# A decoder layer on one core: the order of six branch products, two earlier weight slots, one split inside a norm, and the last scatter

## The reference, cut to what matters

```python
h = rms_norm(x, g_mix)
rq, rk, rv, rg, mq, mk, mv, cq, gl = split(h @ w_in)
o_ret  = rms_norm(retention(rq, rk * RET_DK**-0.5, rv), g_ret_out) * silu(rg)
o_moba = moba_attention(rms_norm(mq), rms_norm(mk), mv)         # 256 tokens: one causal block, ALiBi
mk_, mv_ = split(rms_norm(mem, g_mem) @ w_mem_kv)
o_mem  = softmax(rms_norm(cq) @ rms_norm(mk_).T * MEM_HD**-0.5) @ mv_
gates = sigmoid(gl + b_gate)
y = gates[0] * (o_ret @ w_br_ret) + gates[1] * (o_moba @ w_br_moba) + gates[2] * (o_mem @ w_br_mem)
x = x + y @ w_out

xt = rms_norm(x, g_ffn)
top_v, top_e = top_k(xt @ w_router + b_router, 4); wts = softmax(top_v)
# for each expert e, on the tokens that chose it:
hdn = xt @ w_mlp1[e] + b_mlp1[e]
glu, lin = min(hdn[::2], 7), clip(hdn[1::2], -7, 7)
out = x + sum over e of wts * ((glu * sigmoid(1.702 * glu) * (lin + 1)) @ w_mlp2[e] + b_mlp2[e])
```

## Time and profile before

| | |
|---|---|
| time, median of 3 runs | 1188.52 us (1187.39 to 1189.92) |
| time of the profiled execution | 1189.44 us |
| span of the profiled execution | 1187.5 us |
| TensorE busy | 1147.0 us (97%) |
| VectorE busy | 403.0 us (34%) |
| ScalarE busy | 227.3 us (19%) |
| GpSimd busy | 30.3 us (3%) |
| DMA | 454.86 MB, mean 383 GB/s |
| mean granted TensorE clock | 0.991 |

### The profile page before, as it was taken

The page is one execution under the profiler, slowest core; times in us unless marked ns, Lnnn a source line. Parts: engine busy times, 40 slices in busy tenths (PEclk is TensorE's granted clock), DMA queues, the critical chain, the costliest instruction groups (busy, mean ns, idle before and its releaser), DMA issues.

```text
span 1187.5 us, 13156 instructions
## 1 busy us (share of the span) xinstructions
PE 1147.0 (97%) x5377; PEld 540.3 (45%) x5377; DVE 403.0 (34%) x664; ACT 227.3 (19%) x353; POOL 30.3 (3%) x31
## 2 busy tenths in 40 slices
PE   9999999999999999999999999999999999999998
PEld 8788778874333333333333333333333333333332
DVE  4765666854222222223222322222222222222221
ACT  3545556531000000001011000000000000000001
POOL 0000222100000000000000000000000000000000
PEclk9999999999999999999999999999999999999999
DMA  9765444899999999999999999999999999999996
GB/s 350 273 207 187 151 157 153 317 422 403 421 434 429 432 427 432 430 429 432 429 429 429 429 429 430 428 432 430 428 433 427 428 431 430 427 429 426 429 426 258
DMA packets 46050, 454.86 MB, mean 383 GB/s; under 512 B 3792, under 2 KB 4048, under 8 KB 26736
## 3 DMA queue, kind: packets, MB, share of 16 engines
q1 hardware_dynamic: 45424, 452.60, 91.5%
q10 hardware_dynamic: 576, 1.51, 0.3%
HBM read 453.04 MB, written 1.05 MB: 382 GB/s over the span
## 4 chain that ended last, share of the span: by engine, by line
PE 65%; DMA 31%; DVE 1%; ACT 1%; issue 1%; SPq 1%; DVEq 0%; ACTq 0%
PE PS L1575 23%; PE PS L1366 15%; PE PS L1583 13%; DMA raw<-in_w_mlp 10%; DMA head_raw<-in_w_mlp 7%; DMA value_raw<-in_w_mlp 6%; DMA gate_raw<-in_w_mlp 4%; DMA low_raw<-in_w_mlp 4%; PE PS L1548 3%; PE PS L1619 3%; DMA raw<-in_w_in 1%; PE PS L1397 1%; PE PS L1555 1%; PE PS L1561 1%; PE PS L1606 1%
## 5 line engine op out<-in xcount | busy, mean ns | idle before, releaser
L1269 DVE TENSOR_SCALAR hT<-PS 128x512 f32<-128x512 f32 x32 | 22.1, 691 | 320.9 <-PE PS L1575 320.9
L868 ACT ACTIVATE hT<-hT 128x512 f32<-128x512 f32 x31 | 19.6, 631 | 562.6 <-DVE hT L1269 562.6
L950 DVE TENSOR_TENSOR rest<-raw,mix_hi 128x2048 fp32r<-128x2048 f32 x38 | 90.0, 2371 | 46.5 <-ACT mix_hi L717 46.4
L1575 PE MATMUL PS<-gate_raw,XG 128*64 128x512 f32 x448 | 99.7, 595 | 3.4 <-DMA gate_raw<-in_w_mlp 3.0
L1575 PE MATMUL PS<-value_raw,XG 128*64 128x512 f32 x416 | 95.3, 612 | 4.7 <-DMA value_raw<-in_w_mlp 4.7
L1575 PE MATMUL PS<-low_raw,XG 128*64 128x512 f32 x416 | 92.2, 595 | 2.9 <-DMA low_raw<-in_w_mlp 2.9
L1575 PE MATMUL PS<-raw,XG 128*64 128x512 f32 x384 | 88.2, 613 | 6.8 <-DMA raw<-in_w_mlp 6.8
L1211 DVE TENSOR_TENSOR X<-X,PS 128x512 f32<-128x512 f32 x120 | 74.6, 681 | 57.5 <-PE PS L1619 57.5
L1204 DVE COPY XG<-PS 128x512 f32<-128x512 f32 x32 | 22.1, 691 | 209.8 <-PE PS L1555 209.8
L1575 PE MATMUL PS<-head_raw,XG 128*64 128x512 f32 x384 | 84.9, 594 | 7.5 <-DMA head_raw<-in_w_mlp 7.5
L717 ACT ACTIVATE mix_hi<-raw 128x2048 fp32r<-128x2048 f32 x38 | 72.5, 1913 | 40.0 <-PE PS L1366 30.9
(11 more groups left out here) (264 smaller groups left out, 1302.3 us busy)
## 6 DMA issues: line engine op xcount, KB each, us to landing
value_raw<-in_w_mlp SPq DMA_DIRECT2D x22, 2048.0 KB, 25.8
gate_raw<-in_w_mlp SPq DMA_DIRECT2D x21, 2048.0 KB, 26.0
raw<-in_w_mlp SPq DMA_DIRECT2D x10, 4096.0 KB, 36.4
low_raw<-in_w_mlp SPq DMA_DIRECT2D x19, 2048.0 KB, 24.1
head_raw<-in_w_mlp SPq DMA_DIRECT2D x18, 2048.0 KB, 32.0
value_raw<-in_w_mlp SPq DMA_DIRECT2D x9, 4096.0 KB, 33.0
low_raw<-in_w_mlp SPq DMA_DIRECT2D x9, 4096.0 KB, 35.6
gate_raw<-in_w_mlp SPq DMA_DIRECT2D x9, 4096.0 KB, 37.2
```

Source lines behind the costliest of these rows:

```text
L868: act.activation(sig, glu, ACT.Sigmoid, scale=ALPHA).then_inc(sgm, 1)
L950: dve.tensor_tensor(rest[m % MIX_RING][:, :], raw[m % MIX_RING][:, :], mix_high_part(m)[:, :].bitcast(F32), ALU.subtract)\
L1269: dve.tensor_scalar(glu, PS[:, 0:1024:2], LIMIT, None, ALU.min).then_inc(swi, 1)
L1575: mm = pe.matmul(PS[h * SL:(h + 1) * SL, n * 512:(n + 1) * 512], XG[:, 2 * u + c, :], tile[:, cols], start=False, stop=(u == W1U - 1 and c ...
```

## The change

Five edits, which touch order and place only; what is computed is the same.

- The six branch products: moba0, moba1, ret0, mem0, ret1, mem1 instead of moba0, ret0, mem0, moba1, ret1, mem1. The buffers of the branch outputs are laid out anew, so that both moba outputs, with the values of moba and the gate of retention, lie under slot 7, and the outputs of retention and memory attention under slot 2. The third high buffer (`branch_hi`) lies in the low region, in the place of the memory tokens' high part, and its first use waits only until cv is done.
- First round of slots: slot 8 is issued one unit earlier, slot 7 behind the last branch unit instead of before the last unit of all, with a wait for br_moba1 instead of br_ret1; slot 2 comes before slots 0 and 1, with a wait for br_mem1.
- The split of unit 6, the first of cq, is made inside the evacuation of mq: on ScalarE between the square and the roots, on VectorE between the sum and the reciprocal.
- In the last but one gate slot the split of the next unit stands ahead of the silu step.
- The end: `last_pair` of item 0 for the first 128 tokens stands inside the last down product, the one for the other tokens behind it; the four full products become two pairs. The load of b2 moves from the start of the experts to the load of gffn.

```diff
-BRANCH_ORDER = [(n, br) for n in range(2) for br in ("moba", "ret", "mem")]
+BRANCH_ORDER = [(0, "moba"), (1, "moba"), (0, "ret"), (0, "mem"), (1, "ret"), (1, "mem")]
+EARLY_SPLIT = SPLIT_UNITS[4]
-FIRST_ORDER = (3, 8, 7, 0, 1, 2, 4, 5, 6)
+FIRST_ORDER = (3, 8, 7, 2, 0, 1, 4, 5, 6)
@@ schedule()
+        if not last:
+            steps += splits(GI[g] + 1, (1,))
         if g == "gate4":
             steps += [("silu",)]
-        if not last:
-            steps += splits(GI[g] + 1, (1,))
@@ buffers
+        branch_hi = sb("branch_hi", [P, 2048], F32R, scope=first)
...
+        mix_hi.append(branch_hi)
...
+        oT_homes = {("moba", p): sb(f"oT_moba{p}", [P, 4, S], F32R, scope=mix) for p in range(2)}
         V = {g: sb(f"V_{g}", [P, TT, 512], scope=mix) for g in ("mv", "rg")}
+        oT_homes.update({(br, p): sb(f"oT_{br}{p}", [P, 4, S], F32R, scope=mix) for br in ("ret", "mem") for p in range(2)})
@@ first_round(slot)
                 elif slot == 7:
-                    sp.wait_ge(unit_used, UNITS_DONE[GI["br_ret1"]])
+                    sp.wait_ge(silu_done, 2)
+                    sp.wait_ge(unit_used, UNITS_DONE[GI["br_moba1"]])
...
                 elif slot == 2:
-                    sp.wait_ge(unit_used, max(m for m in SPLIT_UNITS if HI_SLOT[SPLIT_UNITS.index(m)] == MIX_HL) + 1)
+                    sp.wait_ge(unit_used, UNITS_DONE[GI["br_mem1"]])
@@ SP, loop over the units
                 if m == UNITS_DONE[GI["br_moba0"]] + MIX_RING - 1:
                     first_round(FIRST_ORDER[0])
+                if m == UNITS_DONE[GI["br_moba0"]] + MIX_RING:
+                    first_round(FIRST_ORDER[1])
                 if m == UNITS_DONE[GI["br_moba0"]] + MIX_RING + 1:
-                    first_round(FIRST_ORDER[1])
-                if m == N_MIX - 1:
                     first_round(FIRST_ORDER[2])
@@ ScalarE
                 elif k >= SPLIT_3:
-                    act.wait_ge(silu_done, 2)
-                    act.wait_ge(task_done, TASKS[("pv",) + out_block(MOBA_H - 1)] + 1)
+                    act.wait_ge(unit_used, UNITS_DONE[GI["cv"]])
...
                         act.activation(sq.rearrange("p (t n) -> p t n", t=TT), P2, ACT.Square).then_inc(sq_done, 1)
+                        if g == "mq":
+                            mix_high(EARLY_SPLIT)
                         head_roots(g, MOBA_H if g[0] == "m" else MEM_H, MOBA_HD if g[0] == "m" else MEM_HD)
@@ VectorE
                                           AX.X, ALU.add).then_inc(ss_done, 1)
+                        if g == "mq":
+                            mix_low(EARLY_SPLIT)
                         r = reciprocal_roots(g, TT * heads)
@@ TensorE, the end
+            def last_pair(item, t):
+                for n in range(2):
+                    half = (n + item) % 2
+                    rows = slice(half * SL, (half + 1) * SL)
+                    pe.matmul(banks[LAST_BANK[t, n]], STL[rows, n * S + t * P:n * S + (t + 1) * P], (Y, Y2)[n][rows, :],
+                              start=(n == 1 and item == 0), stop=(item == 1)).then_inc(sc_pe if item else last_pair_done, 1)
...
+                    if v == 1 and c == 0:
+                        pe.wait_ge(st_act, j + 2)
+                        pe.wait_ge(yc, j + 1)
+                        last_pair(0, 0)
...
-            last_pair(0)
+            last_pair(0, 1)
             pe.wait_ge(yc, j + 2)
             pe.wait_ge(last_rows, 1)
-            pe.wait_ge(last_pair_done, 2)
-            last_pair(1)
-            for t, n in quarters[2:]:
-                pe.matmul(banks[LAST_BANK[t, n]], STL[:, n * S + t * P:n * S + (t + 1) * P], (Y, Y2)[n][:, :], start=(n == 1), stop=True)\
-                    .then_inc(sc_pe, 1)
+            pe.wait_ge(last_pair_done, 4)
+            for t in range(TT):
+                last_pair(1, t)
```

More of the change, by code:

```diff
@@ L244, in build @@
         first.close()
+        first = ExitStack()
+        branch_hi = sb("branch_hi", [P, 2048], F32R, scope=first)
+        first.close()
         mT = sb("mT", [P, KC, S], scope=low)
@@ L276, in build @@
         o_ret = sb("o_ret", [P, TT, 512], scope=mix)
-        oT_homes["moba", 1] = sb("oT_moba1", [P, 4, S], F32R, scope=mix)
+        sb("b2_rows", [P, D], scope=mix)
         oTp = {br: [oT_homes[br, p] for p in range(2)] for br in ("moba", "ret", "mem")}
@@ L282, in build @@
         head_tile = sb("head_raw", [P, 8192])
-        first = ExitStack()
-        sb("mem_outputs", [P, 2048], scope=first)
-        mix_hi.append(sb(f"mix_hi{MIX_HL}", [P, 2048], F32R, scope=first))
-        first.close()
         value_tile = sb("value_raw", [P, 8192])
@@ L1680, in _ @@
             mm.then_inc(st_pe, 1)
-            quarters = [(t, n) for t in range(TT) for n in range(2)]
             for v in range(W2U):
```

27 lines of the change are left out of this document (9 added, 18 removed).

## The result

| | before | after |
|---|---|---|
| median, 20 runs each, same chip | 1188.83 us (1187.39 to 1190.44) | 1191.03 us (1189.38 to 1192.66) |
| ratio after / before, 95% interval | | 1.0018 (1.0012 to 1.0025) |
| profiled execution: time, span | 1189.44, 1187.5 us | 1191.09, 1189.1 us |
| mean granted TensorE clock | 0.991 | 0.989 |

The kernel is slower by 2.2 us, 0.18%. The forecast was 1188.0, and 1191.03 lies above the range. A profile shows one execution, so small differences between profiles are weaker than the ratios of the medians.

What follows compares the result with a forecast made beforehand. The expert stage was taken as bound by the weight-load queue, its end following TensorE's position at about 300 us. Terms -0.4 - 0.5 + 1.1 - 0.7 = -0.5 us against the median 1188.52 gave 1188.0 us, range 1185.0 to 1190.6.

Steps and rivals of the forecast that it cites:

- Part 1: First norm, 36 to 46 us: TensorE's wait moves ahead of the transposes, 1.5 us; -0.4 us (-2.0 to +0.5).
- one drop in all: Clock: one half-clock drop, at 47 us or moved to 243 us, each costing 1.7 us; chance 0.5.
- rival A: No half-clock drop at all: -0.5 - 1.7 = -2.2 us, giving 1186.3 us; chance 0.23.
- Part 2: Split ahead of silu, 192 to 198 us: TensorE's wait of 0.49 us goes; -0.5 us (0 to -0.5).
- Part 3: Branch order and slots, 205 to 245 us: late w_out weights delay TensorE 1.8 us; +1.1 us at the end.
- The w_out weights land 1.9 to 2.7 us later: First w_out load, behind one more 2 MB load: lands at 232.1 us instead of 230.2, taking 1.9 us.
- So the earlier slots pay back a part: Weight queue after the mixer: shorter by 2 MB, so it ends 0.4 to 1.8 us late; middle taken, +1.1.
- worth little by themselves: Expert weight queue: slots filled earlier gain little, since the end follows TensorE's position at about 300 us; no size given.
- Part 4: The tail: pairs replace full products, TensorE ends at 1183.3 us instead of 1184.1; -0.7 us (0 to -0.85).
- It fits: Last down product: the first pair, 1.11 us, fits inside the 1.13 us wait for weights that ends at 1176.15.
- The load of b2, put at 0: Moved into the mixer, where the queue has gaps: 128 KB, 0.3 us of queue, counted as 0.
- C: Rival, slower: w_out weights 2.7 us late, TensorE waits 2.5 us, clock falls (+1.7); +2.7 us, 1191.2; chance 0.14.

## Why the prediction was wrong

- **Part 1 (early split): right, and the clock went to the better side.** 1.53 us of wait where 1.5 was worked out. All 16 other profiled kernels with the early split waited 1.1 to 1.6 us there and none fell to half clock behind it; the two without it waited 1.98 and 2.43 us and both did. The forecast kept one drop in all with a chance of one half. -0.4 - 1.7 = -2.1 us was in the sum of rival A, and 1.5 us (by the ratio) to 2.0 us (by the medians) were measured.
- **Part 2 (silu): right.** -0.5 forecast, and the wait of 0.5 us is gone. The ratios differ by 0.1% (0.9987 to 0.9977), more than that wait, but each is known only to 0.1%.
- **Part 3 (slots): this is the step that failed.** Its term was +1.1 us; slots 8 and 7 measured +0.26% (3.1 us, from 0.9987 to 1.0013 and from 0.9992 to 1.0018). The mechanism was right and the size was not. "The w_out weights land 1.9 to 2.7 us later ... I take 1.9" holds by bytes: in the changed kernel without repeated waits, clear of the fetch, the load takes 9.4 us, where it takes 7.2 with slots 8 and 7 at their old places, so it is 2.2 us late, with 1.95 us of waits. What had no place in the sum is that the load lands with the slowest of 16 engines, and that filling the gap at 217 us also removes what lets a late engine catch up. In the profiled execution it was 3.6 us late, and the low part of the first half of yT, not only the second y sum, became late too: 3.4 us of waits in place of 1.7. How much of the 3.1 us of the median is bytes and how much late engines stays open.
- **"So the earlier slots pay back a part" was wrong.** The queue was dry from 264.0 to 265.5 us, and TensorE's lateness reached the end in full (+1.43 us at 244 us, +1.46 at 324, +1.6 at the end). By its own first section ("worth little by themselves", the end follows TensorE's position at 300 us) the prediction should have taken the upper bound, 1.8.
- **Part 4 (the end): wrong.** -0.7 forecast; +0.05 to +0.10% measured, and +0.7 us in the profiles. "It fits" took a wait of 1.13 us from one execution; it was 0.3 us in nearly all others, so the pair makes the last down product 0.7 us late. And I followed the chain to the last sum and left out the four stores behind it, which took the gain of 1.0 us back. The load of b2, put at 0, showed no cost that repeats.
- **The rivals.** C gave 1191.2 with "a landing later than 232.5 us". Its landing and size came true (231.59, with TensorE 2.2 us ahead, is 233.8 counted as before), its clock drop of 1.7 us did not: the clock is 1.00 from 240 to 262 us. So its sum comes near 1191.03 by luck, with the end's loss and a larger slot term in place of the drop. It had a chance of 0.14.

The sum by ratios, one kernel after the other: the two splits -0.23%; branch order, slot 2 and b2 +0.10 (to 0.9987; the same step without repeated waits is -0.01 or +0.11, so this term is open to 0.1); slots 8 and 7 with the late engines +0.26 (to 1.0013); the end +0.05. That is the +0.18 measured, as it must be, since each term is the difference of two neighbours; each is known to about 0.1%.

## What to carry to other kernels

A large load that is put in front of a small one which the critical engine waits for can cost its bytes plus the lag of the slowest DMA engine, and a gap in a queue ahead of such a load is not waste. Ask of every earlier load what will run dry later. Before work is moved into a wait, look at that wait in more than one execution: here it was 1.13 us in one and 0.3 in the others. At an end that closes with stores, count from the landing of the last weights to the landing of the last store, since a faster engine in front of the stores may only bunch them.

## What the runs showed of the hardware

- An instruction fetch of 16 KB takes about 1.1 us (1.09 us in the changed kernel). When it fell on a queue without a gap, one engine's end came 1.4 to 1.5 us behind the other 15. It comes once in 27.5 us on the mean (19 to 33 us apart in the changed kernel).
- Engines are late without a fetch too: five of 16, by up to 2 us, in one execution, and one by 2.9 us in another.
- Four stores of 256 KB on two queues take 4.1 us from the first issue to the last landing, whether issued over 1.9 or 0.85 us.
- 48 further wait instructions for a value long reached took TensorE 2.7 to 3.0 us in a row, some 60 ns each; 16 took less than 0.25 us together, and 65 spread over the kernel nothing that can be seen.
- Half clock followed waits of 1.98 and 2.43 us at 44 us, and not one of 2.72 us at 191 us. The length of the wait alone doesn't decide it.
